# Small attentions in column halves with the division ahead of the sum, and a later norm chain at two projection gates

## The reference

```
h = rmsnorm(x, g_mix_pre); z = h @ w_in
ya = conv3(z); yb = pooled means of z             # 256 channels each
yc = 4 heads of 64: causal softmax over the 128 keys chosen by an index score, + relative bias
yd = 4 heads of 64: causal block attention + relative bias
x = x + rmsnorm(concat(ya, yb, yc, yd) @ w_out, g_mix_post)
x = x + rmsnorm((silu(gate) * up) @ w_down, g_ffn_post)      # gate, up = rmsnorm(x, g_ffn_pre) @ w_gate_up
x = x + sigmoid(rmsnorm(x, g_ple) @ w_ple_gate) * (p @ w_ple_proj)
```

## Time and profile before

| | |
|---|---|
| median of 3 runs | 1840.19 us |
| profiled execution: its time, its span | 1842.8 us, 1841.0 us |
| mean granted clock of TensorE | 0.996 |
| PE busy | 1816.1 us, 99% |
| DVE, ACT, POOL busy | 890.4, 607.3, 542.3 us |
| DMA | 177.71 MB, 97 GB/s on average |

### The profile page before, as it was taken

One profiled execution on the slowest core, in us unless ns is written; L12 is line 12 of the kernel. 1 busy time (PEld: TensorE's weight loads), 2 busy tenths in 40 slices (PEclk: granted clock), 3 DMA queues, 4 the chain that ended last, 5 costly groups with the idle time before them and its releaser, 6 DMA issues.

```text
span 1841.0 us, 22183 instructions
## 1 busy us (share of the span) xinstructions
PE 1816.1 (99%) x8622; PEld 1485.0 (81%) x8622; DVE 890.4 (48%) x1226; ACT 607.3 (33%) x875; POOL 542.3 (29%) x346
## 2 busy tenths in 40 slices
PE   9999999999999999999999999999999999999998
PEld 8877788888888877788888888777787788888877
DVE  5556463333335766543333335499656332333366
ACT  4345522222223335422222124234435332222352
POOL 1122255132225430152223245332123220210233
PEclk9999999999999999999999999999999999999999
DMA  6322122222322224225222222312122222232231
GB/s 206 110 81 82 68 92 92 91 92 91 114 91 91 92 94 144 93 92 135 101 96 91 94 100 88 135 67 71 46 81 91 92 91 91 94 112 92 91 115 69
DMA packets 36610, 177.71 MB, mean 97 GB/s; under 512 B 4504, under 2 KB 11448, under 8 KB 17464
## 3 DMA queue, kind: packets, MB, share of 16 engines
q1 hardware_dynamic: 35360, 175.06, 28.0%
q10 hardware_dynamic: 1176, 1.63, 0.7%
HBM read 161.99 MB, written 3.67 MB: 90 GB/s over the span
## 4 chain that ended last, share of the span: by engine, by line
PE 89%; DVE 8%; ACT 1%; DMA 1%; issue 1%; POOL 1%; SPq 0%; DVEq 0%; ACTq 0%
PE ps L532 23%; PE ps L533 23%; PE ps L534 23%; PE ps L575 3%; PE ps L586 3%; PE ps L576 3%; PE ps L789 1%; PE ps L752 1%; PE ps L800 1%; PE ps L1072 1%; DVE xb L1658 1%; PE ps L957 1%; PE ps L967 1%; DVE wlo L1652 1%; DVE idx_score L2098 1%; PE ps L668 1%
## 5 line engine op out<-in xcount | busy, mean ns | idle before, releaser
L1652 DVE TENSOR_TENSOR wlo<-raw,whi 128x2048 fp32r<-128x2048 f32 x135 | 330.2, 2446 | 304.5 <-ACT whi L1192 304.0
L1192 ACT ACTIVATE whi<-raw 128x2048 fp32r<-128x2048 f32 x146 | 278.7, 1909 | 348.1 <-PE ps L534 250.1
L532 PE MATMUL ps<-xb,whi 128*128 128x512 f32 (+1 forms) x996 | 388.4, 390 | 2.0 <-ACT idx_relu L1459 1.3
L534 PE MATMUL ps<-xb,wlo 128*128 128x512 f32 (+1 forms) x996 | 386.1, 388 | 0.0
L533 PE MATMUL ps<-xb,whi 128*128 128x512 f32 (+1 forms) x996 | 386.0, 388 | 0.0
L532 PE MATMUL ps<-xa_hi,whi 128*128 128x512 f32 x788 | 308.7, 392 | 0.9 <-ACT probs L1253 0.7
L534 PE MATMUL ps<-xa_hi,wlo 128*128 128x512 f32 x788 | 306.9, 389 | 0.0
L533 PE MATMUL ps<-xa_lo,whi 128*128 128x512 f32 x788 | 306.8, 389 | 0.0
L532 PEld LDWEIGHTS ps<-xb,whi 128*128 128x128 f32 x996 | 187.1, 188 | 43.2 <-issue 5.5
L534 PEld LDWEIGHTS ps<-xb,wlo 128*128 128x128 f32 x996 | 187.0, 188 | 38.5
L533 PEld LDWEIGHTS ps<-xb,whi 128*128 128x128 f32 x996 | 187.1, 188 | 37.6 <-issue 0.2
(11 more groups left out here) (331 smaller groups left out, 2457.4 us busy)
## 6 DMA issues: line engine op xcount, KB each, us to landing
raw<-wst SPq DMA_DIRECT2D x149, 1024.0 KB, 4.8
stage<-qk_raw SPq DMA_DIRECT2D x32, 128.0 KB, 2.3
h<-xT SPq DMA_DIRECT2D x4, 512.0 KB, 7.5
mla_qn<-q_nope SPq DMA_DIRECT2D x8, 256.0 KB, 2.7
mla_v<-v_tok SPq DMA_DIRECT2D x8, 256.0 KB, 2.7
outT<-h SPq DMA_DIRECT2D x7, 256.0 KB, 2.0
bias_scratch<-bias_rows ACTq DMA_DIRECT2D x1, 1536.0 KB
raw<-wst SPq DMA_DIRECT2D x2, 512.0 KB, 6.2
```

The costliest lines, as they stand in the source:

```text
L532: pe.matmul(out, lhs_hi, rhs_hi, start=first, stop=False)
L534: return pe.matmul(out, lhs_lo, rhs_hi, start=False, stop=last)
L1192: act.activation(whi[slot][:, :], raw[slot][:, :], ACT.Copy).then_inc(whi_done, 1)
L1652: dve.tensor_tensor(wlo[slot][:, :], raw[slot][:, :], whi[slot][:, :].bitcast(F32), ALU.subtract).then_inc(wlo_done, 1)
```

## The change

In the attentions, ACT's new `normalise2` multiplies the probabilities of a job by `rinv` before PE turns them (`transposes` now waits on `pn_done`), DVE's `inverse2` moves ahead for it, and DVE's `normalise2`, `o2` and `turn2` go. The turned tiles of a pair lie in one buffer, `pT_pair`, in which the tiles of one row of keys stand side by side. `weighted2` runs once in a pair, in the odd job: the values are the weights (128x64), the probabilities move (512, 384, 256, 128 columns for the four key tiles), and the two heads write to partitions 0 to 63 and 64 to 127 of one bank. In job 7 it stands behind the pool's matmuls. `min2` is one fused instruction for rows 0 and 1. In the gates, `stat` and `broadcast` move to k-steps 3 and 6 of the second chunk, all adds of the squares go to DVE (`sum_squares`, a first add of 2048 columns), and POOL keeps only the power. The first two output tiles are copied unscaled by ACT (`take_raw`) and scaled by DVE from SBUF (`scale_raw`); ACT makes `whi` of chunk `c+2` in halves. In `proj(1)`, `stat` and `broadcast` stand one tile later each. Everywhere in `features`, the wait for the second tile's bank moves behind the first tile's matmuls of k-step 0.

```
-ADDED = (3, 7, 7, 1, 2, 7, 14, 0, 7, 4, 7, 4)
+ADDED = (3, 7, 7, 1, 2, 7, 14, 0, 7, 3, 7, 3)
...
+def pair_rows(jb, i):
+    return slice(1 + i, 2 + 6 * i, 5) if jb % 2 == 0 else slice(15 - 5 * i, 16 + i, 6)
+def pair_keys(jb, kt):
+    return 1 + 6 * kt if jb % 2 == 0 else 15 - 5 * kt
...
-                    for a in pair:
-                        bank_ready(t0 + a, per, i)
                     for k in range(kt):
...
                         for a in pair:
+                            if k == 0:
+                                bank_ready(t0 + a, per, i)
                             out, m = ps[(t0 + a) % 4][:, :], slice((a_from + a) * P, (a_from + a + 1) * P)
                             if late:
...
                 for j, (w_hi, _) in enumerate(parts):
                     for k in range(KD):
                         if j == 0:
-                            if k == KD - 1:
-                                stat(norm)
                             pe.wait_ge(fresh[1], fresh[2] + k + 1)
                         elif k == 3:
+                            stat(norm)
+                        elif k == 6:
                             broadcast(norm)
                         for a in range(2):
                             out, m = ps[(t0 + 2 * j + a) % 4][:, :], slice(a * P, (a + 1) * P)
...
-            def weighted2(jb):
-                _, _, v, hd = JOBS[jb]
-                n = 2 * HEADS + jb
-                if jb in (0, 4):
-                    for tile in V_TILES[jb // 4]:
+            def weighted2(pair):
+                if pair in (0, 2):
+                    for tile in V_TILES[pair // 2]:
                         pe.wait_ge(bank_free[tile % 4], tile // 4 + 1)
-                pe.wait_ge(on_done, HEADS + jb)
-                for j, i in enumerate(TR_ORDER):
-                    pe.wait_ge(ptc_done, 4 * n + j + 1)
-                    for kt in range(i + 1):
-                        mm = pe.matmul(O_PS[:, i * 64:(i + 1) * 64],
-                                       pT2[:, OFF[i] + kt * P:OFF[i] + (kt + 1) * P],
-                                       v[:, kt, 64 * hd:64 * hd + 64], start=(kt == 0), stop=(kt == i))
+                if pair >= 2:
+                    pe.wait_ge(xl_done, X["mix"] + MIX_PAIR[pair - 2] + 1)
+                pe.wait_ge(ptc_done, 4 * (2 * HEADS + 2 * pair + 2))
+                for kt in range(QT):
+                    for jb in (2 * pair, 2 * pair + 1):
+                        _, _, v, hd = JOBS[jb]
+                        half, first = slice(64 * (jb % 2), 64 * (jb % 2) + 64), pair_keys(jb, kt)
+                        mm = pe.matmul(PAIR_O[pair % 2][half, P * kt:S], v[:, kt, 64 * hd:64 * hd + 64],
+                                       pT_pair[:, first:first + QT - kt, :].rearrange("p k q -> p (k q)"), start=(kt == 0), stop=(kt == QT - 1))
                 mm.then_inc(o_done, 1)
-            def turn2(pair):
-                pe.wait_ge(on_done, HEADS + 2 * pair + 2)
-                if pair:
-                    pe.wait_ge(xl_done, X["mix"] + MIX_PAIR[pair - 1] + 1)
-                for i in range(QT):
-                    mm = pe.transpose(OT[:, i * P:(i + 1) * P], o2[pair % 2][:, i, :], ident[:, :])
-                mm.then_inc(ot_done, 1)
...
-                ready = lambda j, i: (bank_free[T_JOB[jb][i] % 4], T_JOB[jb][i] // 4 + 1)
-                transposes(probs2[PROBS2[jb]], ready, 2 * HEADS + jb, (0, 1, 2))
+                ready = lambda j, i: (pn_done, 4 * (HEADS + jb) + j + 1)
+                transposes(probs2[PROBS2[jb]], ready, 2 * HEADS + jb, (0, 1, 2), jb % 2)
...
-                weighted2(jb)
-                if jb >= 2 and jb % 2 == 0:
-                    turn2((jb - 2) // 2)
...
+                if jb % 2:
+                    weighted2(jb // 2)
                 u = C["att2"] + jb // 2
                 features(u % 2, u, T_PROJ[jb], xb_hi, xb_lo, n=1, a_from=jb % 2)
-            turn2(3)
...
-                features(c % 2, c, t, p_hi, p_lo, kt=2, cols=512, hook=lambda k: stat(8 + 2 * u) if k == 1 else None)
-                features(c % 2, c, t + 2, p_hi, p_lo, kt=2, cols=512, a_from=2,
-                         hook=lambda k: broadcast(8 + 2 * u) if k == 0 else None)
+                features(c % 2, c, t, p_hi, p_lo, kt=2, cols=512,
+                         hook=lambda k: stat(8 + 2 * u) if k == 1 and u == 0 else None)
+                for a in range(2):
+                    if a == u:
+                        broadcast(8 + 2 * u)
+                    elif a < u:
+                        stat(8 + 2 * u)
+                    features(c % 2, c, t + 2 + a, p_hi, p_lo, kt=2, cols=512, n=1, a_from=2 + a)
...
-                    if j == 0 and jb:
-                        act.wait_ge(o_done, n)
-                    act.activation(pT2[:, OFF[i]:OFF[i] + P * (i + 1)], PT[i],
+                    if j == 0 and jb >= 2:
+                        act.wait_ge(o_done, 2 * HEADS + jb // 2)
+                    act.activation(pT_pair[:, pair_rows(jb, i), :], PT[i].rearrange("p (k q) -> p k q", q=P),
                                    ACT.Copy).then_inc(ptc_done, 1)
+            def normalise2(jb):
+                act.wait_ge(ri_done, 2 * HEADS + jb + 1)
+                for i in TR_ORDER:
+                    row = probs2[PROBS2[jb]][:, OFF[i]:OFF[i] + P * (i + 1)]
+                    act.activation(row, row, ACT.Copy, scale=rinv[:, jb % 2, i:i + 1]).then_inc(pn_done, 1)
...
             exp2(0, (2, 3))
+            normalise2(0)
             take_tokens(dv, T_DV[1:2], 1)
...
             for jb in range(8):
                 copy_pT2(jb)
                 if jb < 6:
                     exp2(jb // 2 + 1, (2, 3) if jb % 2 else (0, 1))
+                if jb < 7:
+                    normalise2(jb + 1)
...
+            act.wait_ge(o_done, 2 * HEADS + 4)
             for a in range(2):
...
+            def take_raw(t0):
+                for a in range(2):
+                    act.wait_ge(tile_done, t0 + a + 1)
+                    act.activation(raw_tiles[:, a, :], ps[(t0 + a) % 4][:, :], ACT.Copy).then_inc(bank_free[(t0 + a) % 4], 1)
...
                         if first and s == 0:
-                            hi(c + 2, 0, t + 2)
+                            half_high(c + 2, 0, t + 2)
+                            take_raw(t)
+                            half_high(c + 2, 1, t + 2)
                             take_rstd(9)
-                        act.wait_ge(bank_free[(t + 2 * s) % 4], (t + 2 * s) // 4 + 1 + i)
+                        if first and s == 0:
+                            act.wait_ge(raw_scaled, 2)
+                        else:
+                            act.wait_ge(bank_free[(t + 2 * s) % 4], (t + 2 * s) // 4 + 1 + i)
...
+            def scale_raw(tile, a, tt):
+                dve.wait_ge(bank_free[tt % 4], tt // 4 + 1)
+                dve.tensor_tensor(tile, raw_tiles[:, a, :], rstd_f[:, :], ALU.mult).then_inc(raw_scaled, 1)
...
+                        head, tt, j = NB_HEAD[jb], T_JOB[jb][i], 4 * pair + 2 * (i - 2) + jb % 2
                         b, w0 = ps[tt % 4], P * max(i - 1, 0)
                         tile_ready(tt)
+                        if i < 2:
+                            w = P * (i + 1)
+                            dve.tensor_tensor_reduce(out=b[:, 0:w], in0=b[:, 0:w], in1=nbias[:, head, 2 * P - w:2 * P], scale=1.0,
+                                                     scalar=3e38, op0=ALU.add, op1=ALU.min,
+                                                     accum_out=negmin[:, jb % 2, i:i + 1]).then_inc(nm_done, 1)
+                            continue
...
-            top_rounds(top_at[5], top_at[6])
+            top_rounds(top_at[5], top_at[5] + 1)
+            inverse2(0)
+            inverse2(1)
+            top_rounds(top_at[5] + 1, top_at[6])
             c = C["att2"]
             for jb in range(8):
                 a = jb % 2
-                if a == 0:
-                    inverse2(jb)
-                    inverse2(jb + 1)
                 if jb < 6:
                     min2(jb // 2 + 1, (2, 3) if jb % 2 else (0, 1))
-                normalise2(jb)
+                if jb == 1:
+                    top_rounds(top_at[7], top_at[7] + 1)
+                if jb < 6 and a:
+                    inverse2(jb + 1)
+                    inverse2(jb + 2)
                 if jb < 2:
-                    top_rounds(top_at[6 + jb], top_at[7 + jb])
+                    top_rounds(top_at[6 + jb] + jb, top_at[7 + jb])
...
-                            upper_squares(squares2, 9, 0)
+                            sum_squares(squares2, 9)
+                            lo_halves(c + 2, (0,), 2)
                             mean_square(9, D)
-                            dve.wait_ge(rstd_t_done, 9 + 1)
-                            lo_halves(c + 2, (0,))
                             dve.wait_ge(rstd_f_done, 9)
                         tt = t + 2 * s
+                        if first and isinstance(i, int) and s == 0:
```

(52 more changed lines are left out.)

38 lines of the change are left out of this document (13 added, 25 removed).

## The result

The kernel after takes 1826.22 us (median of 4 runs, 1826.10 to 1826.71), the kernel before beside it 1840.24 us: a ratio of 0.9923, 95% interval 0.9911 to 0.9935, 14.0 us less. The forecast was 1821.2 us, its range 1817 to 1829.5. So the sign and the place of the gains hold, and 5.0 us of the 19.0 are missing.

What follows compares the result with a forecast made beforehand. PE, busy 1816.1 of 1841.0 us, was taken as the bound through its work, waits and clock. Gates 10.0, attentions 8.0 and bank waits 1.0 made 19.0 us, taken from the median 1840.2: 1821.2 us, range 1817 to 1829.5.

Steps and rivals of the forecast that it cites:

- A gate is then 9.43 us: Gates, first low-part matmul to next chunk: PE's 9.09 us of work plus 0.35 us of wait at `broadcast`.
- The sum is 1.2 us early: Gates: DVE's new sum is done at 1427.9, PE asks at 1429.1, so no idle time and no clock fall.
- The rival that the gates do not gain: Gates: `x_lo` stays at 1.05 us, sum 1.9 us late, idle and clock fall stay; near 1831 us; chance 0.10.
- the term, 10.0 us: Gates: 14.60 + 14.58 - 2 x 9.43 = 10.3 us saved, less 0.3 us charged in the second projection.
- the terms are differences, so they are taken from the median: Whole kernel: 19.0 us taken from the median 1840.2, though the profiled execution took 1842.8 us.
- 0.3 us was charged: Second projection, `proj(1)`: `broadcast` and the DVE work after it start 0.5 us later, delaying the first `xb_hi` tiles.
- The attentions: 8.0 forecast: Small attentions: 18.9 us removed, 10.0 added, 1.35 of stalls, 0.4 of today's small waits; bounds 11 and 1.4 us.
- the four terms: Attentions, new stalls of PE: 0.5 us in job 0, 0.2 in job 2, 0.25 in job 4, 0.6 at the pool.
- series: Rival, pair's sum in the attentions: column halves run in series, 6.6 us less gained, 1828 us; chance 0.15.
- bare loads: Rival, pair's sum: in series, and 64 records each pay 0.05 to 0.10 us more, 1831 to 1834 us; chance 0.03.
- a part of 0.10 us for each of eight steps: Pair's sum: 2.07 + 8 x 0.10 = 2.9 us; 64 columns may need half that load, so 2.5 taken.
- The bank waits: 1.0 forecast: `features`, second of two banks: at most 2.0 us of waits go, DVE takes some back in the index stage; 1.0 taken.

Runs made afterwards that it cites:

- `old_sum`: The kernel after with the old sum of squares in both gates (three adds on POOL, then three on DVE), `stat` and `broadcast` at the new places: 1826.79 us.
- `take_first`: The kernel after with DVE's scaling of the tile in jobs 2 and 4 put ahead of the two low parts in its queue: 1823.97 us.
- `halves_in_series`: The kernel after with the eight matmuls of a pair's sum issued head by head instead of in turn: 1832.47 us.

## Why the prediction was right, and where the 5 us went

- **What bounds the kernel**: right. What PE lost to waits, clock and work is what came back, and no other engine became the bound.
- **The gates: time.** "A gate is then 9.43 us": 9.37 and 9.36. "The sum is 1.2 us early": 1.2. `x_lo`, taken at 0.663 us: 0.67. The rival that the gates do not gain fell twice over, for even with POOL's adds and the old order of adds kept (`old_sum`) PE waits for the sum only 0.26 us.
- **The gates: the term, 10.0 us, is the first that was mis-sized: 6.1 measured.** The step that failed is "the terms are differences, so they are taken from the median". It holds for work, not for a loss that differs from run to run. Of the 29.2 us that both gates took in that execution, 5.9 were falls of the clock (twice 14.60 less 11.66); an ordinary run has 2.6 us less (1842.8 less 1840.2), which I read and did not connect with the falls. The clock's part of the two gates was too large by about these 2.6 us; the next point has most of the rest.
- **Behind the first gate** 1.1 us of the saving was lost. By milestones (the start of one and the same matmul in both traces) PE was 12.2 us ahead of the kernel before at the end of the gate (1438.69 and 1426.50) and 11.1 us in the fourth chunk, whose high part ACT made only at 1434.00, behind a hidden tile of POOL. No part of the prediction looked past "the next chunk". In the second projection 0.3 us was charged, and 0.28 us of the lead was lost from there to the second gate.
- **The attentions: 8.0 forecast, 6.3 measured.** Better: 2.31 for 2.5 us a pair, 0.8 in all, and mostly slightly smaller stalls in jobs 0, 2 and 4 (0.51, 0.12 and 0.17 us for 0.5, 0.2 and 0.25) and at the pool (under 0.3 for 0.6; the four terms are 1.55, where the text has 1.35). Worse: the waits in jobs 3 and 5, 2.5 us by `take_first`, and 0.45 us at `w_out`'s second chunk. I listed what queues on PE and on ACT behind a late division, and did not follow it to DVE: ACT's `whi` comes later behind the division, DVE's `lo` waits for it, and a `take_scaled` whose input came 0.2 us after the start of `lo` stands behind it for 2.6 us.
- **The column halves**: right that they run side by side, and the rivals of series and of bare loads are ruled out. The price of the step was not: the forecast took a part of 0.10 us for each of eight steps, from the score pair, and no step of the pair costs more than a head's own (0.43, 0.32 and 0.22 us, as in line 967 of the kernel before). The 0.24 us over the 2.07 stand at the ends: 0.05 in the first step (0.48 for 0.43) and 0.18 behind the last record (0.21 to the next chunk, for 0.03). That 2.5 came near 2.31 is in part luck. The Trainium skill, TensorE: Matmul & The Clock Gate, on packing small matmuls, has weight loads overlap a running matmul only when the row group differs. Both heads here have the same 128 rows, and in both orders a weight load of 0.14 us begins within 0.01 us of the start of a matmul that runs for 0.27 to 0.64 us (the matmul at 1302.21, the load at 1302.22). The trace does not agree with the rule for this stream.
- **The bank waits: 1.0 forecast, 2.6 measured** by themselves. In the kernel after, the milestones gave 0.95; the index stage did take part of it back (L1047 waits 1.1 us for DVE). The rest, 2.6 less 1.4 us of waits, may be the clock of single runs, as above; it is not shown.
- **Sum**: 6.1 + 6.3 + 2.6 = 15.0 against 14.2 measured together. One reason may be that a fall of the clock that one part removes can't be removed again by another; the 0.8 us are within the intervals of the parts, so this is argued and not shown. What is not settled: why a pause of 2 us is followed by none, 3.41 or 6.83 us at half speed, and why a wait of 0.6 or 0.7 us in the index stage could have one beside it, when the wait of 1.5 us behind the second projection of the kernel after had none (its clock is 1.00 in every window up to the very end).

## What to carry to other kernels

When the mean clock of the profiled execution is below that of other runs, price the clock's part from several executions: here one gate took 11.7, 13.0 or 14.6 us. When an engine gets more work, follow each in-order queue behind it one engine further than the one that waits, and past the end of the stage that is being mended; four changes of order of single instructions were worth 4.3 us here, beside the 14.0 of the whole change. And the place where a result is asked for can be worth more than how fast it is made: at the new place the faster sum is worth 0.37 us a gate, while asking for it eight matmuls earlier, against the order of DVE's queue, costs 6.5 us in the two gates, the clock's part included.

## What the hardware showed

- The falls of the clock came in two lengths only, 3.41 and 6.83 us, at 0.50 of full speed, in every profiled execution that had one (nine of 3.41, three of 6.83, those at the very end of a program left out).
- Two matmuls in column halves of the array, fp32, the same 128 rows, written to the two partition halves of one bank, start 6 to 8 ns apart. The 16 records take 2.31 us, and one head's eight take 2.30 us (`halves_in_series`), so the second half costs nothing. Head by head the two take 3.86 us, 1.67 times as long, with an overlap of 0.74 us at the seam (2 x 2.30 less 3.86).
- POOL's adds beside DVE slow `x_lo` from 0.67 to 1.06 us on average (8.51 us for eight before), yet with `stat` at the new place that was worth 0.37 us a gate.
